# Four edits to a one-core encoder layer: uncleared FFN sum with a PSUM end, a table of conv taps, ada sums in three chunks, one table set for the head norm

## What is computed

```python
mod = silu(c) @ w_ada + b_ada                # 6 vectors of 1024: sh1 sc1 gt1 sh2 sc2 gt2
h = rms_norm(x, g_pre_mix) * (1 + sc1) + sh1
zin = h @ w_in                               # 3072 columns
cv_val, cv_gate, q, f, i, og = split(zin)    # 6 x 512
out_a = silu(layer_norm(causal_depthwise_conv31(cv_val * sigmoid(cv_gate)) + b))
out_b = hgrn2(q, f, i, og, lb, norm_g)       # 4 heads of 128: gated linear recurrence, rms norm per head
mix = concat(out_a, out_b) @ w_out
x = x + gt1 * rms_norm(mix, g_post_mix)
h2 = rms_norm(x, g_pre_ffn) * (1 + sc2) + sh2
gate, up = split(h2 @ w_ffn_in)              # 2 x 2816
y = (silu(gate) * up) @ w_ffn_out
x = x + gt2 * rms_norm(y, g_post_ffn)
```

## Time and profile before

| | us |
|---|---|
| median of 3 runs | 1297.75 (1297.48 to 1300.44) |
| profiled execution, its own time | 1305.6 |
| its span in the trace | 1303.5 |
| TensorE busy | 1214.9 (93%), mean granted clock 0.978 |
| VectorE busy | 606.4 (47%) |
| GpSimd busy | 444.0 (34%) |
| ScalarE busy | 295.4 (23%) |

### The profile page before, as it was taken

One profiled execution on the slowest core, in us unless ns is written; L12 is line 12 of the kernel. 1 busy time (PEld: TensorE's weight loads), 2 busy tenths in 40 slices (PEclk: granted clock), 3 DMA queues, 4 the chain that ended last, 5 costly groups with the idle time before them and its releaser, 6 DMA issues.

```text
span 1303.5 us, 14392 instructions
## 1 busy us (share of the span) xinstructions
PE 1214.9 (93%) x5754; PEld 1013.5 (78%) x5754; DVE 606.4 (47%) x679; ACT 295.4 (23%) x450; POOL 444.0 (34%) x237
## 2 busy tenths in 40 slices
PE   0599999999989699979999999999999999999995
PEld 0488888888878588768888888888888888888874
DVE  5926996969976564732212121212121212121228
ACT  2624245262521734330000000000000000000013
POOL 1344433334232630513242424242424242424235
PEclk9899999999989899979999999999999999999998
DMA  9334232233110150102121212121212111212103
GB/s 381 123 89 121 81 95 83 81 98 95 51 33 17 57 186 1 49 1 65 33 64 32 64 32 64 32 64 32 64 32 64 32 64 32 64 32 64 33 17 129
DMA packets 84471, 89.76 MB, mean 69 GB/s; under 512 B 2541, under 2 KB 72402, under 8 KB 83410
## 3 DMA queue, kind: packets, MB, share of 16 engines
q1 hardware_dynamic: 84146, 87.16, 20.7%
q10 hardware_dynamic: 288, 2.10, 0.4%
HBM read 85.05 MB, written 4.19 MB: 68 GB/s over the span
## 4 chain that ended last, share of the span: by engine, by line
PE 86%; DVE 9%; ACT 3%; issue 1%; DMA 0%; SPq 0%; POOL 0%; DVEq 0%; ACTq 0%
PE pair L1117 54%; PE pair L1220 23%; PE pair L1152 4%; PE pair L1277 2%; DVE tail_tmp L1008 1%; DVE acc L782 1%; DVE y L989 1%; DVE x L772 1%; DVE full L810 1%; DVE hb_lo L986 1%; PE pair L1148 1%; PE pair L1166 1%; DVE xs L772 1%; PE pair L1105 1%; PE pair L1090 1%
## 5 line engine op out<-in xcount | busy, mean ns | idle before, releaser
L486 POOL CAST w_hi<-raw 128x1024 fp32r<-128x1024 f32 x60 | 62.5, 1041 | 438.5 <-PE pair L1117 254.2
L1038 DVE TENSOR_TENSOR ufull<-gate,pair 128x1024 f32<-128x1024 f32 x22 | 26.9, 1221 | 394.7 <-PE pair L1117 381.9
L1117 PE MATMUL pair<-ha_hi,w_hi 128*128 128x512 f32 x528 | 169.7, 403 | 5.3 <-DVE hb_lo L802 5.3
L1117 PE MATMUL pair<-hb_hi,w_hi 128*128 128x512 f32 x528 | 166.2, 396 | 0.0
L1117 PE MATMUL pair<-ha_lo,w_hi 128*128 128x512 f32 x528 | 164.8, 394 | 0.0
L1049 DVE TENSOR_TENSOR yt<-yt,pair 128x1024 f32<-128x1024 f32 x88 | 107.4, 1221 | 123.4 <-PE pair L1220 123.4
L1117 PE MATMUL pair<-ha_hi,w_lo 128*128 128x512 f32 x528 | 164.4, 393 | 0.0
L1117 PE MATMUL pair<-hb_lo,w_hi 128*128 128x512 f32 x528 | 163.0, 390 | 0.0
L1117 PE MATMUL pair<-hb_hi,w_lo 128*128 128x512 f32 x528 | 162.6, 389 | 0.0
L847 DVE SCALAR_TENSOR_TENSOR pair<-u,conv_w_col,pair 128x512 f32<-128x512 f32 x240 | 162.1, 750 | 0.9 <-DVE state L923 0.2
L488 POOL TENSOR_TENSOR w_lo<-raw,w_hi 128x1024 fp32r<-128x1024 f32 x60 | 154.0, 2566 | 4.8
(11 more groups left out here) (184 smaller groups left out, 1538.5 us busy)
## 6 DMA issues: line engine op xcount, KB each, us to landing
raw<-in_w_ffn_in SPq DMA_DIRECT2D x44, 512.0 KB, 3.7
ada<-in_w_ada SPq DMA_DIRECT2D x32, 512.0 KB, 3.8
raw<-in_w_in SPq DMA_DIRECT2D x24, 512.0 KB, 3.6
raw<-in_w_ffn_out SPq DMA_DIRECT2D x22, 512.0 KB, 3.3
x<-in_x SPq DMA_DIRECT2D x8, 1024.0 KB, 15.3
ada<-in_w_ada SPq DMA_DIRECT2D x6, 1024.0 KB, 12.1
raw<-in_w_out SPq DMA_DIRECT2D x8, 512.0 KB, 3.2
out<-x SPq DMA_DIRECT2D x8, 512.0 KB, 2.6
```

The source lines that it names most:

```text
L486: pool.tensor_copy(w_hi[:, j % WS, :], raw[:, j % RAW, :]).then_inc(loop_hi, 1)
L1038: dve.tensor_tensor(ufull[:, :], gate[:, :], pair[1][:, :], ALU.mult).then_inc(ufull_ready, 1)
L1117: i_ = pe.matmul(dst[:, cols], w, x[:, cols], start=first and s_ == 0, stop=last and s_ == 2)
```

## The change

1. `yt` isn't cleared. VectorE's first FFN block is peeled off its loop and copies the tiles from PSUM to `yt` instead of adding.
2. `down` waits for each of its two weight splits and `u` parts where it first uses them, not for both ahead.
3. At the end the gains stay in PSUM (`pair[0]`), and VectorE reads them there. ScalarE's squares go to `pair[1]` and no longer wait for GpSimd. The product waits for GpSimd's add three tiles back. For the last tile VectorE multiplies by the gains first and, when the root is there, scales and adds in one instruction.
4. The taps follow tables: 40 behind `gated` (one per piece up to 25, two up to 33, three at 34 to 36, then two) and 22 in the next period (3, 3, 2, 2, then one per piece; in the last period ten times two, then one and one).
5. The ada products and sums stand in the last three chunks of a period: j = 0, 1 in the third, 2, 3, 4 in the fourth, 5, 6, 7 in the fifth. ScalarE places them at the third, fifth and seventh piece of the chunk.
6. In front of the head norm's Ln there is a preload of the set `natural_log_exp_and_others`.

```diff
-ADA_OPS = [(0,), (1, 2), (3, 4), (5, 6), (7,)]
-TAPS_FIRST = 37
+ADA_OPS = [(), (), (0, 1), (2, 3, 4), (5, 6, 7)]
+
+TAPS_BEHIND = [0] * 17 + [1] * 9 + [2, 2, 2, 2, 2, 2, 2, 2, 3, 3, 3, 2, 2, 2]
+TAPS_LEFT = [3, 3, 2, 2] + [1] * 12
+TAPS_LEFT_LAST = [2] * 10 + [1, 1]
...
-            pool.wait_ge(w_used, G0)
-            pool.memset(yt[:, :, :], 0.0).then_inc(yt_zero, 1)
...
                     if half:
+                        act.preload_act_table_set("natural_log_exp_and_others")
                         act.wait_ge(ss_head, TT * (t + 1))
...
-                    if period < 4 and k in (3, 5):
-                        for j in ADA_OPS[c][(k - 3) // 2:(k - 1) // 2]:
+                    if period < 4 and k in (2, 4, 6):
+                        for j in ADA_OPS[c][(k - 2) // 2:k // 2]:
                             product(KT * period + j)
...
-                if i >= 2:
-                    act.wait_ge(tail_done, TT + i - 1)
-                tail_norm(yt[:, i, :], i % 2, i)
+                tail_norm(yt[:, i, :], pair[1][:, :], i)
...
+                behind = sum(TAPS_BEHIND)
                 if period < 4 and piece > U_AT:
-                    per = TAPS_FIRST
-                    a, b = ((piece - U_AT - 1 + x) * per // (39 - U_AT) for x in (0, 1))
-                    base = 2 * TAPS * period
+                    base, table, at = 2 * TAPS * period, TAPS_BEHIND, piece
                 else:
-                    length = U_AT if period < 4 else 12
-                    if period == 0 or piece >= length:
+                    table = TAPS_LEFT if period < 4 else TAPS_LEFT_LAST
+                    if period == 0 or piece >= len(table):
                         return
-                    per = 2 * TAPS - TAPS_FIRST
-                    a, b = ((piece + x) * per // length for x in (0, 1))
-                    base = 2 * TAPS * (period - 1) + TAPS_FIRST
-                for n in range(base + a, base + b):
+                    base, at = 2 * TAPS * (period - 1) + behind, piece
+                for n in range(base + sum(table[:at]), base + sum(table[:at + 1])):
                     tap(n)
...
-            def scaled_product(i, src, slot, count):
+            def scaled_product(i, src, slot, count, gain=ggb):
...
+                if first:
+                    dve.tensor_copy(yt[:, i, :], pair[2 + i % 2][:, :]).then_inc(y_added, 1)
+                    return
                 dve.tensor_tensor(yt[:, i, :], yt[:, i, :], pair[2 + i % 2][:, :], ALU.add).then_inc(y_added, 1)
...
-            dve.wait_ge(yt_zero, 1)
-            with dve.Fori(0, FB - 1) as bk:
+
+            def ffn_block(bk, first=False):
...
+            ffn_block(0, first=True)
+            with dve.Fori(1, FB - 1) as bk:
+                ffn_block(bk)
...
-            dve.tensor_copy(ggb[:, :], pair[0][:, :]).then_inc(ggb_ready, 1)
-            dve.wait_ge(ggb_ready, 2)
-
-            for i in range(TT + 1):
-                if i < TT:
-                    add_tile(FB - 1, i, 6 * (FB - 1) + F0 + 6)
+
+            for i in range(TT):
+                add_tile(FB - 1, i, 6 * (FB - 1) + F0 + 6)
                 if i:
-                    scaled_product(i - 1, yt[:, i - 1, :], (i - 1) % 2, TT + i)
-            dve.wait_ge(tail_read, 2 * TT)
-            dve.tensor_tensor(x1[:, TT - 1, :], x1[:, TT - 1, :], tail_tmp[:, (TT - 1) % 2, :], ALU.add
-                              ).then_inc(last_done, 1)
+                    if i >= 3:
+                        dve.wait_ge(tail_done, TT + i - 2)
+                    scaled_product(i - 1, yt[:, i - 1, :], (i - 1) % 2, TT + i, pair[0])
+            i = TT - 1
+            dve.wait_ge(y_added, FB * TT + CREDIT)
+            dve.wait_ge(tail_done, TT + i - 1)
+            me.done(dve.tensor_tensor(tail_tmp[:, i % 2, :], yt[:, i, :], pair[0][:, :], ALU.mult))
+            dve.wait_ge(tail_ss, TT + i + 1)
+            me.done(dve.reciprocal(rs[:, 1, i:i + 1], rs[:, 1, i:i + 1]))
+            me.wait()
+            dve.scalar_tensor_tensor(out=x1[:, i, :], in0=tail_tmp[:, i % 2, :], scalar=rs[:, 1, i:i + 1],
+                                     in1=x1[:, i, :], op0=ALU.mult, op1=ALU.add).then_inc(last_done, 1)
...
             def down(bk, need, slot):
-                pe.wait_ge(w_split, need + 2)
-                pe.wait_ge(u_ready, bk * 2 + 2)
...
+                        if i == 0:
+                            pe.wait_ge(w_split, need + f + 1)
+                            pe.wait_ge(u_ready, bk * 2 + f + 1)
```

More of the change, by code:

```diff
@@ L251, in build @@
         y_added = sem("y_added")
-        yt_zero = sem("yt_zero")
         out_stored = sem("out_stored")
@@ L702, in _, with tail_norm @@
             mix_high(7, ot[:, 3, :])
-            def tail_norm(src, slot, i):
-                root_mean_square(src, tail_tmp[:, slot, :], i, 1, D).then_inc(tail_ss, 1)
+            def tail_norm(src, junk, i):
+                root_mean_square(src, junk, i, 1, D).then_inc(tail_ss, 1)
             def x1_norm(i):
@@ L712, in _ @@
                 act.wait_ge(w_used, N_IN + i + 1)
-                tail_norm(out_pair(i)[:, :], 1, i)
+                tail_norm(out_pair(i)[:, :], tail_tmp[:, 1, :], i)
                 x1_norm(i)
@@ L1007, in scaled_product @@
                 me.wait()
-                dve.scalar_tensor_tensor(out=tail_tmp[:, slot, :], in0=src, scalar=rs[:, 1, i:i + 1], in1=ggb[:, :],
+                dve.scalar_tensor_tensor(out=tail_tmp[:, slot, :], in0=src, scalar=rs[:, 1, i:i + 1], in1=gain[:, :],
                                          op0=ALU.mult, op1=ALU.mult).then_inc(tail_read, 1)
@@ L1042, in u_low, with add_tile @@
                 dve.tensor_tensor(u_lo[:, slot, :], ufull[:, :], u_hi[:, slot, :], ALU.subtract).then_inc(u_ready, 1)
-            def add_tile(bk, i, used):
+            def add_tile(bk, i, used, first=False):
                 if i < TT - 1:
@@ L1048, in add_tile, with add_down @@
                     dve.wait_ge(w_used, used)
+                if first:
+                    dve.tensor_copy(yt[:, i, :], pair[2 + i % 2][:, :]).then_inc(y_added, 1)
+                    return
                 dve.tensor_tensor(yt[:, i, :], yt[:, i, :], pair[2 + i % 2][:, :], ALU.add).then_inc(y_added, 1)
-            def add_down(bk, used):
+            def add_down(bk, used, first=False):
                 for i in range(TT):
-                    add_tile(bk, i, used)
+                    add_tile(bk, i, used, first)
             F0 = N_IN + N_OUT
@@ L1061, in _ @@
                 u_full(bk * 2 + 2, bk * 6 + (F0 + 6))
-                add_down(bk, bk * 6 + (F0 + 8))
+                add_down(bk, bk * 6 + (F0 + 8), first)
                 u_low(bk * 2 + 2, 0)
+            ffn_block(0, first=True)
+            with dve.Fori(1, FB - 1) as bk:
+                ffn_block(bk)
             u_full(FFT - 1, 6 * (FB - 1) + F0 + 4)
```

## The result

The changed kernel takes 1317.97 us (median of 4 runs, 1315.13 to 1318.96); four runs of the kernel before, on the same chip, have a median of 1299.10 (1297.48 to 1304.99). The medians lie 18.9 us apart. The ratio of the two sets of runs is given as 1.0124, with an interval of 1.0088 to 1.016: slower, by some 16 us (11 to 21), above the +9.5 of the prediction. The two profiled executions differ by less: 1305.6 before (span 1303.5) and 1315.13 after (span 1313.4), +9.9 in the spans. Both numbers are true, for the kernel before has executions near 1297.5, near 1302 and near 1306, and its profiled one was of the last kind; experiments 4 and 5 show what makes the last kind.

The account below looks back on a forecast made before the run. TensorE bounds the kernel, with ScalarE tight at changes of period. Loss 28.5 less gains 6.3 + 6.5 + 6.2 = 19.0 gives +9.5 us: 1307 on the median of 1297.75 (about 1315 for the profiled execution), range 1292 to 1317.

Parts of the forecast that it names:

- The losing part: Three ada chunks at changes of period: product 7 waits for its load, stopping TensorE 19.6 us; 28.5 lost in all.
- One sum: Change of period 0 to 1: end of sum 5, put at 121.5, leading to a stop of 3.2, taken as 3.5.
- the clock: Slow TensorE behind stops at changes of period: 2.5 each for three and 0.8 for the last, 8.3, between 3 and 12.
- Rival 2: Changes of period: the wait comes but the clock hardly falls, 19.6 + 1 - 19.0, so 1299; chance 0.15.
- rival 3: Changes of period: clock takes 3.4 each time and the level multiplication is held, +14.9, 1313; chance 0.13.
- The level multiplication: Last one (piece 25): GpSimd's moved sums hold it up to 0.8 in three periods, 0 to 2.4; 0.6 taken.
- One table set: LayerNorm before the output projection: three table loads go, multiplications run ahead; gain 6.3, between 5.5 and 7.2.
- No clearing: Head of the FFN: without GpSimd's memset xs(6) and xs(7) come earlier; gain 6.5, between 5.0 and 7.7.
- The end: Last eight output tiles: gains in PSUM, products 1.28, adds 2.72 apart; gain 6.2, between 5.0 and 7.5.
- Taps: VectorE's taps moved between pieces by the table: zero taken, bounds a loss of 4.2 and a gain of 0.7.
- Rival 1: Product 7 at changes of period: the ring wait stays hidden, no loss, 1279; chance 0.15.
- The last sentence of the prediction: Changes of period: the prediction is wrong if one costs under 4.7 us.

Follow-up runs that it names:

- experiments 4 and 5: Kernel before with one part each: set 0.9949, no clearing 0.9956, end 0.9953, taps 0.9990; then reprofiled unchanged (1297.97), memset forced after (1301.38) or before (1305.63) tile-6 norm.
- experiments 1 to 3: Changed kernel without ada part 0.9828; ada part alone in kernel before 1.0244; changed kernel with three-place ada ring 0.9925, four chunks 0.9834, three groups one chunk earlier 0.9863.
- experiment 5: Kernel before profiled again unchanged: 1297.97; memset held until tile 6's norm: median 1301.38; that norm held until the memset ends: median 1305.63.
- four chunks: Changed kernel with ada products and sums two by two in the first four chunks of a period, none in the fifth: 1281.68, ratio 0.9834.

## Why the prediction came out as it did

**The losing part: right in place, chain and sign.** The prediction said that product 7 waits for a turn of the ring of 6.4 us, with the OT and V copies queued behind it. The turn in the profile after runs from the end of product 5 (about 381.8) to 387.92: 6.1. The stops of TensorE were put at 3.5, 5.2, 5.2 and 5.7; measured are 3.5, then 3.05 + 1.72 = 4.8, 2.99 + 1.72 = 4.7, and 4.38 - 0.91 = 3.5, the wait of rows 2 taken off. Idle time 16.4 against 19.6. ScalarE's idle time before the product is 4.38 where "some 4.5" was named, and experiments 1 to 3 show that nothing else loses. One sum has a slip: 117.5 + 2.0 + 2.4 is 121.9, not 121.5. With it the first stop comes out 0.4 longer, at 3.6; since 3.5 was taken and 3.50 measured, nothing hangs on it.

**The term that was mis-sized: the clock, 8.3 against some 12.5.** I took 2.5 for each of the first three changes, the middle of two rows, and only 0.8 for the last. The windows give 3.4, 3.4 and 1.7 for the three, 8.5 where I had 7.5, and 5.7 - 1.7 = 4.0 for the last. The step that failed is the 0.8: I took the 1.7 that the last change pays already from a price made for short stops, and behind a stop of 4.38 the clock stood at 0.50 for ten microseconds. Nor is that 1.7 a fixed part of the kernel before: its second profile doesn't pay it (experiment 5). The sum lies just beyond the 12 that I had as the upper bound. Rival 2, that the clock would hardly fall, is out, and rival 3 (3.4 each, levels held, 1313) was the closest picture of this part: 11.9 + 2.4 against 12.5 + 2.3.

**The level multiplication: 0.6 against 2.3.** The bound of 2.4 was right, up to 0.8 in each of three periods; the list has 2.3, 3 times, at most 0.8. The sum of chunk 3 starts 0.12 us ahead of it:

```profile
356.42 2.42 POOL L456 TENSOR_TENSOR acc<-acc,ada 128x1024 f32<-128x1024 f32 x1
356.54 3.39 DVE L875 TENSOR_TENSOR qk<-qk,tt 128x1024 f32<-128x1024 f32 x1 [2.02 <-PE pair L1159]
```

Both instructions follow from the same schedule in every period, and the hold came in each of the three; the 0.6 between "never" and "always" was no likely outcome. The rule of the Trainium skill that was weighed there (SBUF — State Buffer, "Who interferes with whom") was right with its worst case.

**One table set: 6.3 against 7.0.** Right, including that one load is all that a head has. The Trainium skill (ScalarE: Activation LUTs, "What ACT_TABLE_LOAD costs") puts a switch at about 2.66 us, a load of 1.28 and some 1.38 of draining; the trace doesn't agree with the second part, since the instruction ahead of the load ends at 376.91, the load runs from 376.93 to 378.21, and Ln begins at 378.22.

**No clearing: 6.5 against 8.0 in the profiles, and about 0 to 2 in the executions that the median of the runs stands for.** This is the step that failed as a forecast of the median. The rows were read rightly, and the chain through xs(6) and xs(7) is the one that went, though xs(6) takes 1.16 and not the 0.75 that was named as a sign. But I moved a gain taken from an execution of 1305.6 onto a median of 1297.75 with the words "the same 9.5". The 7.9 us between the two, which I had called 0.6%, were nearly all this very loss: 7.6 lie between the two profiles of that kernel. An execution of 1297.5 has no 6.31 to give back. For it the sum of the measured terms is 31.6 - 7.0 - 6.9 = 17.7, less at most 1 or 2 of gain from the clearing, so 1313 to 1315 from 1297.5, against the profiled 1315.13. The runs after lie at 1315 to 1319, with a median 3 to 5 above this sum; what these are is open, since the changed kernel was profiled once. The forecast for the profiled execution, "about 1315", met 1315.13, and that is in part luck: the loss was put 3.1 too low (28.5 against 31.6) and the gains 2.9 too low (19.0 against 21.9), and the two errors cancel. The 1307 for the median was 11 too low: 7.9 for this reason, and 2.8 because the median after lies that far above its own profiled execution.

**The end: 6.2 against 6.9,** with products of 1.28, adds 2.72 apart and the last add held, as said. **Taps: 0 against 0** (0.999, 0.9967 to 1.0014).

**Rival 1,** the ring wait hidden, 1279: out for this change, but the time is what one gets where the wait is really hidden. Without the ada part 1280.86 was measured, and 1281.68 with four chunks. The changed kernel with the products left where they were is the best version found, at 0.9828 of before, the four chunks equal to it within the intervals. The last sentence of the prediction set a limit of 4.7 us for a change of period; all told they cost 31.6 / 4 = 7.9, net of what the preload saves there.

## What to carry to other kernels

Before one moves work in a queue that runs in order, one follows the buffer that the work needs through its whole turn (consumer, the engine that frees it, the issuing queue, the landing), and asks who stands behind it in the queue at the new place: the same three groups cost 34 us in one place and 4 to 6 a chunk earlier. A stop of TensorE in a stage without slack is to be counted with the slow clock behind it, here two thirds as much again (12.5 on 18.7 of idle time). When the profiled execution is as far from the median of the runs as here (0.6%), one should look for what differs between the executions before adding a gain read from the one to the other.

## What the runs showed of the hardware

A near tie between two engines can give a kernel several times. GpSimd's split and VectorE's add were issued 0.02 to 0.16 us apart, in either order from one execution to the next; who came first ran at full speed (2.40, 1.22) and the other waited (3.46, 3.44), and a memset that only writes held VectorE's scaling for 6.31. Through the norms behind them this made 7.6 us of 1300, and a wait on a semaphore that fixes the order of memset and norm takes most of the spread away: 1297.9 to 1302.6 with one order, 1305.3 to 1307.0 in nine of ten runs with the other. The Trainium skill (SBUF — State Buffer, "Who interferes with whom") says that issue order decides who blocks; the trace agrees, in both orders of the same two instructions.

TensorE's clock falls behind short stops, but not every time. Behind 3.50, 3.05 + 1.72, 2.99 + 1.72 and 4.38 us of waiting, stretches of 10 to 15 us held 1.2 GHz for part of the time or all of it, and 3.4, 3.4, 1.7 and 5.7 us of work were lost. Behind equal stops (3.05 + 1.72 and 2.99 + 1.72) it was 3.4 and 1.7, and behind the same wait of 0.91 in two executions of one kernel the clock was 0.66 over 5 us in one and 1.00 in the other. I can't say from these runs what makes the difference; a price of the clock read from one profile may be off by the whole 1.7 for each such stop.
